# Output biases moved from the late expert pairs to the third, and a resident weight chunk of the second pair instead of a late one

## The reference

```python
h = x + concat([att, conv_out]) @ w_out          # (320, 1024)
x2d = rms(h, norm2_g)
logits = x2d @ w_router + b_router               # 32 experts
top_logits, top_idx = top_k(logits, 4)
gates = softmax(top_logits)
for each expert e, for the tokens routed to it:
    gu = xe @ w_gu[e] + b_gu[e]                  # 1024 -> 2048
    g, u = min(gu[:, :1024], 7), clip(gu[:, 1024:], -7, 7)
    hid = (u + 1) * (g * sigmoid(1.702 * g))
    y += gate * (hid @ w_down[e] + b_down[e])    # 1024 -> 1024
return h + y
```

## Time and profile before

| | |
|---|---|
| median of 3 runs | 1072.7 us (1072.42 to 1074.67) |
| the profiled execution's own time | 1072.61 us |
| its span | 1070.9 us |
| mean granted TensorE clock | 0.988 |
| TensorE matmuls busy | 1029.8 us, 96% |
| VectorE busy | 317.6 us, 30% |
| ScalarE busy | 95.9 us, 9% |
| moved by DMA | 420.30 MB, mean 392 GB/s |

### The profile page before, as it was taken

The page is one execution under the profiler, slowest core; times in us unless marked ns, Lnnn a source line. Parts: engine busy times, 40 slices in busy tenths (PEclk is TensorE's granted clock), DMA queues, the critical chain, the costliest instruction groups (busy, mean ns, idle before and its releaser), DMA issues.

```text
span 1070.9 us, 11705 instructions
## 1 busy us (share of the span) xinstructions
PE 1029.8 (96%) x5098; PEld 491.2 (46%) x5099; DVE 317.6 (30%) x491; ACT 95.9 (9%) x165; POOL 8.3 (1%) x20
## 2 busy tenths in 40 slices
PE   8999999999999999989898989989898989999998
PEld 7767454444444444435343534434353435334333
DVE  3533031323323232312313231323223232313243
ACT  2222040100000000000001010000000000100001
POOL 1100000000000000000000000000000000000000
PEclk9999999999999999999999999999999999999999
DMA  9950969999999999999999999999999999999996
GB/s 353 317 117 1 376 232 405 419 423 424 425 420 430 427 428 428 431 427 427 430 430 427 427 430 430 427 428 428 429 428 430 427 429 429 428 415 420 422 421 256
DMA packets 57470, 420.30 MB, mean 392 GB/s; under 512 B 21061, under 2 KB 21377, under 8 KB 28257
## 3 DMA queue, kind: packets, MB, share of 16 engines
q1 hardware_dynamic: 56848, 419.32, 94.7%
q0 software_dynamic: 352, 0.55, 0.2%
q10 hardware_dynamic: 240, 0.03, 0.0%
HBM read 418.29 MB, written 1.58 MB: 392 GB/s over the span
## 4 chain that ended last, share of the span: by engine, by line
PE 71%; DMA 28%; SPq 0%; issue 0%; DVE 0%; ACT 0%; DVEq 0%
PE ps L896 35%; DMA ring<-in_w_gu_dram 27%; PE ps L912 7%; PE ps L820 7%; PE ps L741 5%; PE ps L938 3%; PE ps L759 3%; PE ps L617 2%; PE ps L923 1%; PE ps L898 1%; PE ps L770 1%; PE ps L942 1%; PE ps L1074 1%; PE ps L643 1%; PE ps L709 0%; DMA x<-in_x_prompt_dram 0%
## 5 line engine op out<-in xcount | busy, mean ns | idle before, releaser
L896 PE MATMUL ps<-ring,xT 128*64 128x512 f32 x1008 | 457.2, 607 | 29.0 <-DMA ring<-in_w_gu_dram 28.7
L898 PE MATMUL ps<-ring,xT 128*64 128x512 f32 x1008 | 457.7, 608 | 0.0
L896 PEld LDWEIGHTS ps<-ring,xT 128*64 128x64 f32 x1008 | 135.8, 139 | 304.4 <-issue 300.1
L912 PE MATMUL ps<-ring,he 128*64 128x512 f32 x480 | 214.2, 595 | 3.9 <-DMA ring<-in_w_down_dram 3.0
L914 PE MATMUL ps<-ring,he 128*64 128x512 f32 x472 | 211.0, 596 | 0.0
L1667 DVE TENSOR_TENSOR x<-ps,x 128x512 f32<-128x512 f32 (+1 forms) x84 | 54.3, 684 | 295.7 <-PE ps L938 268.0
L898 PEld LDWEIGHTS ps<-ring,xT 128*64 128x64 f32 x1008 | 135.9, 139 | 0.0
L912 PEld LDWEIGHTS ps<-ring,he 128*64 128x64 f32 x480 | 62.8, 137 | 133.5 <-issue 133.2
L820 PEld LDWEIGHTS ps<-oh,hn 128*128 128x128 f32 x720 | 89.5, 196 | 8.2 <-issue 6.0
L820 PE MATMUL ps<-oh,hn 128*128 128x128 f32 x720 | 91.4, 282 | 0.0
L1309 ACT COPY gu_sb<-ps 128x1024 f32<-128x1024 f32 x16 | 16.2, 1012 | 596.0 <-PE ps L898 596.0
(11 more groups left out here) (233 smaller groups left out, 633.0 us busy)
## 6 DMA issues: line engine op xcount, KB each, us to landing
ring<-in_w_gu_dram SPq DMA_DIRECT2D x102, 2048.0 KB, 25.8
ring<-in_w_down_dram SPq DMA_DIRECT2D x50, 2048.0 KB, 27.0
ring<-in_w_gu_dram SPq DMA_DIRECT2D x48, 1024.0 KB, 15.5
ring<-in_w_down_dram SPq DMA_DIRECT2D x25, 1024.0 KB, 25.3
w_chc<-in_w_in_dram SPq DMA_DIRECT2D x1, 4096.0 KB, 21.1
w_qkv<-in_w_in_dram SPq DMA_DIRECT2D x4, 768.0 KB, 9.0
w_b<-in_w_in_dram SPq DMA_DIRECT2D x1, 2048.0 KB, 28.9
w_o<-in_w_out_dram SPq DMA_DIRECT2D x2, 1024.0 KB, 28.1
```

The lines of the kernel that those rows point to most:

```text
L896: even = mm(gu_banks(j)[0:CAP, n, :], xT[j % 2][:, k, 0:CAP], first[n], start=(k == 0), stop=(k == KT - 1))
L898: odd = mm(gu_banks(j)[CAP:P, n, :], xT[j % 2][:, k, CAP:P], second[n], start=(k == 0), stop=(k == KT - 1))
L912: even = mm(out[0:CAP, half, :], hid[:, f, 0:CAP], first[2 * a + half], start=(f == 0), stop=(f == FT - 1))
```

## The change

`BIASED` becomes all six units of the sums of pair 0, which are scattered in pair 2. With it go to pair 2: turning the gates after k = 0, ScalarE's copy of them, and the waits for it and for `b_dn`, both at k = 1. For this the rooms of `b_dn` and `gatesT` must be free by then, so `PIECES_AT` becomes (3, 3), read at k = 3 of pair 1; behind its use follows the load of `b_dn`. Chunk (28, 0) goes through the ring like the others and (3, 3) no longer does. Since one chunk fewer of the early ones is in the ring, `slot_of(n)` is n modulo 16 instead of n + 1, and the first loads are written in that order. The loop on TensorE covers pairs 4 to 13 in five turns, and pairs 0 to 3 are written out.

```diff
-        BIASED = {PAIRS - 4: (2, 3, 4, 5), PAIRS - 3: (0, 1)}
+        BIASED = {0: range(2 * NT)}
...
-        EARLY_AT, LATE_AT, PIECES_AT = (1, CH - 1), (NE - 2, 0), (NE - 4, 0)
+        EARLY_AT, LATE_AT, PIECES_AT = (1, CH - 1), (NE - 2, 0), (3, 3)
...
         def slot_of(n):
-            return (n + 1) % RING
+            return n % RING
...
-            two = (EARLY - 3 <= n < RINGED + 1 - FINE and c % 2 == 0 and ORDER[n + 1] == (e, c + 1)
+            two = (EARLY - 4 <= n < RINGED + 1 - FINE and c % 2 == 0 and ORDER[n + 1] == (e, c + 1)
                    and slot_of(n) < RING - 1)
...
-            load(*ORDER[RING - 1], 1, slot_of(RING - 1))
-
-            FIRST_DONE = RING - 2
-            for n in range(RING - 2):
+            FIRST_DONE = RING - 1
+            for n in range(RING - 1):
                 slot = slot_of(n)
...
-            IN_LOOP, PER_LOOP = range(2, PAIRS - 2), 2 * 2 * CH
+            IN_LOOP, PER_LOOP = range(4, PAIRS - 2), 2 * 2 * CH
...
-            GROWING = ([(value, 2) for value in range(1, 6)] + [(value, 2 * 2 * NT) for value in range(2, 2 * 2 * NT + 1, 2)]
+            GROWING = ([(value, 2) for value in range(3, 8)]
+                       + [(2 * 2 * NT + value, 2 * 2 * NT) for value in range(2, 2 * 2 * NT + 1, 2)]
                        + [(value, PER_LOOP // RING * 16) for value in ARRIVALS])
...
-                    if j == PAIRS - 2 and k == 0:
+                    if j == 2 and k == 0:
                         turn_gates()
...
                             pe.wait_ge(yl_ready, so_far(j, j - 1, 2))
-                            if j == PAIRS - 2:
+                            if j == 2:
                                 pe.wait_ge(gatesT_ready, 1)
+                                pe.wait_ge(b_down_in, 16)
                         else:
-                            if j == PAIRS - 2:
-                                pe.wait_ge(b_down_in, 16)
                             pe.wait_ge(added, so_far(j, 2 * NT * (j - 2) + k - 1, 2 * 2 * NT))
...
-            pair(0)
-            pair(1)
+            for j in range(IN_LOOP[0]):
+                pair(j)
...
-                if j == PAIRS - 2:
+                if j == 2:
                     act.wait_ge(gates_turned, 1)
                     nc.scalar.copy(gatesT[:, :], GT).then_inc(gatesT_ready, 1)
```

## The result

The changed kernel takes 1082.7 us (median of 6 runs, 1081.15 to 1084.04) where the kernel before, run beside it, takes 1073.45 us (6 runs). The ratio is 1.0091, 95% interval 1.0080 to 1.0101: it is slower by 9.8 us, 8.6 to 10.8. The profiled execution took 1082.77 us for a span of 1080.9, 10.0 us longer than before. The prediction was 1080.4 us and +7.7, in a range of 1075.5 to 1082.5: the sign and the place were right, the size was 2 us short, and the median lies 0.2 us outside the range. The forecast of the time started from 1072.7 us; the kernel before, in the runs beside, stood 0.75 us above that, so the measure of the forecast is the +9.8 against its +7.7.

What follows compares the result with a forecast made beforehand. The unbroken weight stream was taken as the bound: 8.9 us lost in pair 2, less 1.1 us of slack, gave +7.8, with -0.3 bias table and +0.2 code +7.7, so 1080.4 us, range 1075.5 to 1082.5.

Steps and rivals of the forecast that it cites:

- What bounds the kernel: From about 164 us the unbroken stream of expert weights; taking work off TensorE in pairs 14 and 15 saves 1.1 us.
- The price of the biases and of the gates' transposes: Six biases in three groups, 2.5, 2.5 and 2.3 us, plus 0.5 us of transposes: 7.8 us moved to pair 2.
- The first two gaps: Pair 2, loads (6, 0) and (6, 2) released late: 5.1 us of stream lost by the first, 8.9 us in all.
- s: Time a load must be issued before the last one lands to avoid a gap: 2.7 to 3.6 us, taken as 3.2.
- no further gap: The load after (6, 2), issued at 300.0 us, more than s before the one ahead lands, loses nothing.
- The shorter queue by itself: From chunk (3, 3) to pair 14 one ring chunk fewer on order, each landing due 2.45 us earlier.
- The end: Last weight halves land 8.9 us later, at 1068.7, and are used 0.1 us later: +7.8 us, tail as before.
- The bias table: Its 128 KB leave the late stream and go where the stream has gaps: -0.3 us.
- D: Rival: the late stage pays too, by a clock fall in the last steps or instruction loads; 1082 to 1084 us, chance 0.08.
- The loop and the order of loading: Loop from the fifth pair and new order of the first 16 slots: 0 each; added instruction loads +0.2 us.
- The fixed part by the Trainium skill: About 2.0 us fixed per load by that page; with it the sum would be 1.2 us lower.

Runs made afterwards that it cites:

- e3: The kernel before with the output biases left out altogether; 1072.9 us, ratio 1.0000 to the kernel before.
- e7: The changed kernel with only the biases of units 0 and 1 in pair 2, those of units 2 to 5 in pair 14; 1077.64 us.
- e1: The changed kernel with its biases put back to pairs 14 and 15, resident chunk and loop as changed; 1074.85 us.
- e4: The changed kernel with the biases in pair 4 instead of pair 2 and the loop from the seventh pair; 1074.81 us.
- e6: The changed kernel with 5 more, overwritten products of y_hi in each scatter unit of pair 2; 1089.45 us.
- e9: The changed kernel with one-chunk instead of two-chunk loads in pairs 1 to 3; 1080.94 us.

## Why the prediction was right, and where it fell short

*What bounds the kernel.* Right. The biases taken away altogether change nothing (e3), and the span follows the landing of the last weights in thirteen kernels.

*The price of the biases and of the gates' transposes.* Right, 3.4 and 6.45 us a group in pair 2 as in the late pairs; (6, 0) and (6, 2) were issued within 0.4 us of the times forecast.

*The first two gaps.* Right by the landings: 8.7 us lost by (6, 2), forecast 8.9.

*The step that failed* is the next sentence: "the load ahead of it lands at 303.5, which is more than s later, so no further gap". (6, 4) was issued at 300.3, and the load ahead landed at 291.2 + 12.1 = 303.3, so 3.0 us later. It landed at 310.1, 6.8 us behind that one, with 4.9 us of data: 1.9 us more were lost. The term that was mis-sized is s, put at 2.7 to 3.6 us from the two loads of the earlier trace rows. For loads issued shortly before the one ahead landed the traces show more: 9.8 - 4.9 = 4.9 us for (6, 4), issued 3.0 us before; 10.1 - 4.9 = 5.2 in e7, issued 3.5 us before. The two rows were also too few for the engines at rest: the first ring load of the kernel before, issued at 161.3 us, 5.9 us after the one ahead had landed, took 6.7 us for one chunk, s = 4.2, while the same load of the changed kernel took 5.1, s = 2.7. So the upper bound of s was too low. But s is not one number near 5 either: by the earlier trace rows the load issued at 282.7 us, 4.6 us before the one ahead landed, lost nothing (9.5 - 4.9 = 4.6). With 4.9 for the third gap alone the sum is +9.6.

*The shorter queue by itself.* The sum has no cost for it ahead of (6, 0), yet there are small holes at 212 and 252 us, and without biases in pair 2 it stays at about +2 us (e1, e4). It does not come on top of the 8.7 us: (6, 0) went out 0.7 us before the load ahead of it landed (278.1) and (6, 2) 0.7 us after the one ahead of it had (290.1), so by this reading their issue times alone set their landings. e6 bears it out: (6, 2) issued 6.7 us later, and 6.75 us at the end.

*The end.* The slack of 1.1 us gave back 0.4: the landing moved by 10.7 and the use by 10.3. From 1055.6 us on TensorE has a chain of steps and scatters without a wait, and took the last halves up 0.6 us after they landed. The tail behind the last scatters was 0.3 us shorter, which gives the span's +10.0.

*The bias table.* -0.3 was given for it. By the windows of the kernel before and of e1, which differ in where the table is loaded, it is more:

```profile
925.00:950.00 25.00, 22.59 (x97) 8.42 (x95) 4.93 (x5) 1.58 (x2) 0.52 (x1) 0.93 1.01 414
...
925.00:950.00 25.00, 22.26 (x95) 7.81 (x97) 5.25 (x6) 1.58 (x2) 0.00 (x0) 0.93 1.00 427
```

25 x (427 - 414) / 428 = 0.8 us, an estimate. And it did not go where the stream has gaps of its own, but to 209.9 us, into the short queue.

*The rivals.* The time is the one given for D, but not by D's cause: the granted clock is 1.00 in every window that I took from 950 to 1074 us, and 0.93 from 925 to 950 us in both kernels. TensorE waits for ring loads in the late pairs as forecast, 10.2 us in all where there were 2.4.

*The loop and the order of loading.* "0" for both and +0.2 for the code. The instruction loads rose from 20 to 25, as forecast. The costs are not settled: 0.8 us for the loop and 1.0 us for chunk and order, each with 0 in its interval.

*The fixed part by the Trainium skill*, page "DMA: Bandwidth & Descriptors", section "Anatomy of one DMA — SWDGE (gpsimd) path": about 2.0 us. Here it is 2.7 to 4.2 us with the engines at rest and up to 5.2 with the queue about to run out; the measurement decides, for these loads from SP.

## What to carry to other kernels

Where weights come as one unbroken stream, ask of each piece of compute not which engine it burdens but when it lets go of a buffer: the same 7.8 us cost nothing in pairs 4, 14 or 15 and 7.9 us in pair 2, where each load was issued only some 9 to 16 us before it landed. The number to read is the time from issue to landing, place by place, less the load's own transfer; when that is near the load's fixed part, TensorE's work passes through to the end one to one, though TensorE never waits there. And take the fixed part from several loads, also from such as were issued to a queue about to run dry, not from two with the engines at rest.

## What I had not expected of the hardware

A two-chunk load issued 3.0 and 3.5 us before the one ahead landed was slower (9.8 and 10.1 us) than one issued after all had landed (7.6 us). The trace says where that time sits. It holds sixteen arrivals for each load, and the landing is the last of them. Those of (6, 2) in the changed kernel, which went out to engines at rest, lie within 0.8 us (297.6 to 298.4), those of (6, 4) within 2.1 us (308.0 to 310.1); before the change those of (6, 2) lie within 2.6 us (289.6 to 292.2). From the load ahead of (6, 4) to (6, 4) the mean of the sixteen moves by 5.6 us (303.0 to 308.6) for 4.9 us of data. So 0.7 of the 1.9 us is lost on all, and 1.2 us is the last arrivals falling behind again. By the means, (6, 2) is already 10.0 us late (298.1 against 290.6 - 2.45) and (6, 4) 10.2 us: going out to engines at rest put its arrivals into step, and that hid 1.4 us of the first two gaps in the landing of (6, 2). Why some arrivals fall behind stays open.

In e9 the granted clock fell to 0.67 in the window at 268 us with TensorE busy 4.00 of 4.00 us in it and in the window before; no wait stands ahead of it. What TensorE did just before were scatters with bias products (32 rows deep); what it did then is the gather behind them, which took 4.51 us here and 3.02 us in the changed kernel. The same stands in e4 behind the bias products of pair 4:

```profile
370.00:373.00 3.00, 3.00 (x8) 1.04 (x8) 0.69 (x1) 0.00 (x0) 0.00 (x0) 1.00 1.01 431
...
374.00:376.00 2.00, 2.00 (x11) 2.00 (x11) 0.09 (x1) 0.00 (x0) 0.00 (x0) 0.50 1.00 426
```

The fall at 940 us stands behind a wait for the stream; one in e7 (0.65 from 958 to 960 us) again follows bias products. Each was seen in one execution. The changed kernel has the same bias products with 1.00 in every window from 252 to 340 us, so what brings the fall on isn't settled.
